# Seven-product tiles: product 1 copied into the next bank and accumulated on, products in another order

## The chip, the cores and the metric

The kernel runs on 1 core of one Trainium2 chip. The metric is the device time of one execution in microseconds, lower is better. Engines are named as in the profile: PE (TensorE matmul), PEld (its weight loads), DVE (VectorE), ACT (ScalarE), POOL (GpSimd), SP (SyncE, which issues the weight loads from memory).

## The reference, cut

A streaming encoder of two layers on 640 tokens (512 of a prompt, 8 streams of 16), width 1024, all in fp32. Each layer is a half SwiGLU feed-forward, a token mixer (retention in the first layer, stick-breaking attention in the second), a second half SwiGLU, and a gated per-layer embedding. The change lies in the up-projections of the feed-forward:

```python
def half_swiglu(x, g, w_gu, w_down):          # D_MODEL 1024, D_FF 2816
    h = rmsnorm(x, g) @ w_gu
    a, b = jnp.split(h, 2, axis=-1)
    return x + 0.5 * ((jax.nn.silu(a) * b) @ w_down)
```

It is called four times (`w_ffn_a` and `w_ffn_b` of both layers).

## The kernel before, in words

Activations lie transposed in SBUF: 128 partitions, 8 blocks of the model width, 640 token columns (`TOK`), which are handled as two halves of 320 (`HALF`). A matmul of fp32 precision is made of three in fp32r: each operand is split into a high part (ScalarE copies it, rounding: `w_hi`, `x_hi`, `g_hi`) and a low part (VectorE subtracts: `w_lo`, `x_lo`, `g_lo`), and high x high, high x low and low x high are summed in PSUM.

A feed-forward works through its 22 blocks of hidden units in four pieces of 4, 6, 6 and 6 (`PIECES`). For a piece it computes the blocks' `silu(a) * b`, then 8 down-projections (`KT`) that add the piece to `x`. The first piece uses plain products (L481). The other three use seven products in place of eight, in Winograd's form of Strassen's scheme: for a tile the 2x2 blocks are (gate weights, up weights) x (two halves of the model width) against (two halves of the width) x (two halves of the tokens). A tile is one block of 128 hidden units with both its gate and its up part. `winograd(piece)` runs six tiles, one after the other; there are 3 stages in each of 4 feed-forwards, 12 stages and 72 tiles. A product is 12 matmuls of 128x128 by 320 columns (4 blocks of width x 3 splits), all issued by `product` at L547. Operands of products 5, 6 and 7 are sums of weight blocks (`w_sum`, VectorE's `s1_s2`, `s3`, `s4`) and of activation blocks (`t_hi`, `t_lo`); each weight block, summed or not, is split again by ScalarE (`hi12`, `hi56`, `hi7`, `hi3`, `hi4`) and VectorE (`lo12`, `lo56`, `lo7`, `lo3`, `lo4`) just ahead of its product.

A tile has three PSUM banks, `x`, `y` and `v`, and the next tile the other bank pairs; the outputs are made so:

- product 1 into `x`; product 2 into `v`; the first result (gate, first half of tokens) is their sum: ScalarE's `snap1` copies `x` to SBUF, VectorE's `c11` adds `v` to it
- product 6 adds to `x`; `snap2` copies that (products 1 + 6) to SBUF
- product 5 into `y`; `snap3` copies it; product 7 adds to `x`, and `c22` adds `snap3`'s copy: the up part, second half
- product 3 adds to `y`, and `c12` adds `snap2`'s copy: the gate part, second half; product 4 adds to `x`: the up part, first half
- `silu` over all 640 columns, `gated` multiplies by the up part (two multiplications of 320 columns each), `ghi` and `glo` split the result for the down-projections

Products 3 and 4 of a tile are issued inside the next tile (`third(old)`, `fourth(old)`), so a middle tile's order on TensorE is 1, 2, 3old, 6, 4old, 5, 7; the first tile of a stage has 1, 2, 6, 5, 7; behind the last one stand its own 3 and 4.

Each engine runs a program written out by hand, in order; engines wait for each other by semaphores only. A wait stops all that stands behind it in the same engine's queue. ScalarE's queue in a tile is snap1, hi12 (of the next tile), hi3, snap2, silu (old), hi4, ghi (old), snap3, hi56 and hi7 (next). VectorE's is c22 (old), lo56, lo7, s1_s2 (next), c11, s3 (next), lo12 (next), c12 (old), lo3, gated (old), s4 (next), lo4, glo (old). Raw weights come by DMA into a ring of four slots (`raw`); SP issues slot n when the low split of slot n - 4 is done (`s_wlo`), so lo7 and lo4 release loads. Product 1 of a tile waits for `s_free`, which `gated` of the tile before increments.

Lines of the profile that matter: L547 the products; L481 the ordinary matmuls; L1071 snap1, L1076 snap2, L1080 snap3, L1084 silu, L1040 hi12, L1061 hi3, L1065 hi4; L1688 c11, L1693 c12, L1698 and L1700 gated, L1639 s1_s2, L1655 lo12, L1675 lo4; L1561 the low split of ordinary weights, L1566 that of activations.

Of the kernel before, what the change touches and what calls it, by code (L numbers as in the profile page):

```python
# [30 lines left out]
TOK = SEQ + STREAMS * STEP  # L31
TT = TOK // P
HALF = TOK // 2
# [19 lines left out]
CREDIT = 4  # L53
# [145 lines left out]
def trunk(nc, phases, xT, pT, gains, wst, ones_d, ident_d, negtri_d, cs_d, dec_d, rmask_d, smask_d, gpow_d,  # L199
          bmask_d, bcap_d, st_d, kc_d, vc_d, y_o, stp_o, sts_o, k_o, v_o):  # L200
    F, R = mybir.dt.float32, mybir.dt.float32r
    ALU, ACT = mybir.AluOpType, mybir.ActivationFunctionType
# [3 lines left out]
    with ctx:  # L206
        def sb(name, shape, dt=F, on=ctx):
            return on.enter_context(nc.sbuf_tensor(name, shape, dt))


        x = sb("x", [P, KT, TOK])
# [8 lines left out]
        scr = sb("scr", [P, 4, TOK])  # L220
# [68 lines left out]
        def sem(name):  # L289
            return ctx.enter_context(nc.semaphore(name))  # L290
# [16 lines left out]
        s_silu, s_sig, s_gate, s_tri = sem("s_silu"), sem("s_sig"), sem("s_gate"), sem("s_tri")  # L307
# [5 lines left out]
        s_free = sem("s_free")  # L313
        s_turned = sem("s_turned")
        s_wlo, s_xlo, s_rstd, s_glo, s_plo = sem("s_wlo"), sem("s_xlo"), sem("s_rstd"), sem("s_glo"), sem("s_plo")
        s_sr, s_xup, s_out = sem("s_sr"), sem("s_xup"), sem("s_out")
        s_rt, s_rot, s_kvs = sem("s_rt"), sem("s_rot"), sem("s_kvs")
# [4 lines left out]
        s_prod = {n: sem(f"s_prod{n}") for n in (1, 2, 3, 5, 6, 7)}  # L322
        s_read = sem("s_read")
        s_snap1, s_snap2, s_snap3 = sem("s_snap1"), sem("s_snap2"), sem("s_snap3")
        s_hi12, s_hi56, s_hi3, s_thi = sem("s_hi12"), sem("s_hi56"), sem("s_hi3"), sem("s_thi")
        s_lo12, s_lo56, s_lo3, s_tlo = sem("s_lo12"), sem("s_lo56"), sem("s_lo3"), sem("s_tlo")
        s_sum = [sem(f"s_sum{n}") for n in range(1, 5)]
        s_c11, s_c12, s_c22 = sem("s_c11"), sem("s_c12"), sem("s_c22")
        s_xn, s_t = sem("s_xn"), sem("s_t")

        s_apart, s_unshift = sem("s_apart"), sem("s_unshift")
# [61 lines left out]
        def w_block(wide, extra, n):  # L393

            return wide[:, n // 2, BLK * (n % 2):BLK * (n % 2 + 1)] if n < 4 else extra[:, n - 4, :]
# [10 lines left out]
        def b_side(product, whole, extra):  # L406

            at_x = {1: (0, 0), 2: (1, 0), 3: (1, 1), 4: (0, 1)}
            return quarter(whole, *at_x[product]) if product < 5 else extra[:, product - 5, :, :]
# [63 lines left out]
        def _(pe):  # L473
# [45 lines left out]
            def ffn(c):  # L519
# [19 lines left out]
                def product(n, out, start):  # L539

                    at = {1: 4, 2: 5, 3: 3, 4: 2, 5: 0, 6: 1, 7: 6}[n]
                    wh, wl = w_block(w_hi, wx_hi, at), w_block(w_lo, wx_lo, at)
                    xh, xl = b_side(n, x_hi, t_hi), b_side(n, x_lo, t_lo)
                    for k in range(4):
                        w = slice(k * P, (k + 1) * P)
                        for q, (a, b) in enumerate(((wh, xh), (wh, xl), (wl, xh))):
                            last = nc.tensor.matmul(out, a[:, w], b[:, k, :], start=start and k == 0 and q == 0,  # L547
                                                    stop=k == 3 and q == 2, skip_group_check=True)
                    return last

                def split_up_to(operand):

                    order = ("T1", "T3", "T2", "B11", "B21", "B22", "T4")
                    pe.wait_ge(s_tlo, CREDIT + 7 * (c["g"] // sum(PIECES)) + order.index(operand) + 1)

                def third(d):

                    pe.wait_ge(s_lo3, CREDIT + d["q"] + 1)
                    pe.wait_ge(s_snap3, CREDIT + d["q"] + 1)
                    product(3, d["y"], False).then_inc(s_prod[3], 1)  # L560
# [7 lines left out]
                def winograd(piece):  # L568
                    old = None
                    for d in fast_pairs(c, piece):  # L570
                        start_of = piece == 1 and d["first"]
                        pe.wait_ge(s_lo12, CREDIT + d["q"] + 1)
                        pe.wait_ge(s_free, CREDIT + c["unit"] + 1 + d["m"] - 2)
                        if start_of:
                            split_up_to("B11")
                        product(1, d["x"], True).then_inc(s_prod[1], 1)
                        if start_of:
                            split_up_to("B21")
                        product(2, d["v"], True).then_inc(s_prod[2], 1)
                        if old:  # L580
                            if old["first"] and piece == 1:
                                split_up_to("B22")
                            third(old)
                        pe.wait_ge(s_lo56, CREDIT + d["q"] + 1)
                        pe.wait_ge(s_snap1, CREDIT + d["q"] + 1)
                        product(6, d["x"], False).then_inc(s_prod[6], 1)
                        if old:
                            if old["first"] and piece == 1:
                                split_up_to("T4")
                            fourth(old)  # L590
                        product(5, d["y"], True).then_inc(s_prod[5], 1)
                        pe.wait_ge(s_wlo, CREDIT + c["n"] + d["m"] + 1)
                        pe.wait_ge(s_snap2, CREDIT + d["q"] + 1)
                        product(7, d["x"], False).then_inc(s_prod[7], 1)
                        old = d
                    third(old)
                    fourth(old)
# [365 lines left out]
        def _(act):  # L963
# [44 lines left out]
            def ffn(c):  # L1008
# [58 lines left out]

                def snap1(d):
                    act.wait_ge(s_prod[1], CREDIT + d["q"] + 1)
                    act.wait_ge(s_c11, CREDIT + d["q"])  # L1070
                    nc.scalar.activation(scr[:, 2, HALF:TOK], d["x"], ACT.Copy).then_inc(s_snap1, 1)  # L1071

                def snap2(d):
                    act.wait_ge(s_prod[6], CREDIT + d["q"] + 1)
# [5 lines left out]
                    nc.scalar.activation(scr[:, 2 + d["par"], 0:HALF], d["y"], ACT.Copy).then_inc(s_snap3, 1)  # L1080

                def silu(d):
                    act.wait_ge(s_c12, CREDIT + d["q"] + 1)
                    nc.scalar.activation(scr[:, d["par"], :], scr[:, d["par"], :], ACT.Silu).then_inc(s_silu, 1)  # L1084

                def ghi(d):
                    act.wait_ge(s_free, CREDIT + o + d["m"] + 2)
# [457 lines left out]

        @block.vector
        def _(dve):
            for s in (*s_sum, s_lo12, s_lo56, s_lo3, s_tlo, s_c11, s_c12, s_c22, s_xn, s_t, s_turned, s_free, s_wlo, s_xlo, s_rstd, s_glo, s_plo, s_sr, s_xup, s_out, s_rt, s_rot, s_kvs,
                      s_aggr, s_gn, s_ylo, s_sp, s_llo, s_cap, s_gated):
                dve.sem_inc(s, CREDIT)  # L1550
            tt, ts, stt = nc.vector.tensor_tensor, nc.vector.tensor_scalar, nc.vector.scalar_tensor_tensor
# [42 lines left out]
            def ffn(c):  # L1594
# [86 lines left out]
                    out = scr[:, 2 + d["par"], 0:HALF]  # L1681
                    tt(out, d["x"], out, ALU.add).then_inc(s_c22, 1)

                def c11(d):
                    dve.wait_ge(s_prod[2], CREDIT + d["q"] + 1)
                    dve.wait_ge(s_snap1, CREDIT + d["q"] + 1)
                    dve.wait_ge(s_glo, CREDIT + d["f"] - 1)
                    tt(scr[:, d["par"], 0:HALF], d["v"], scr[:, 2, HALF:TOK], ALU.add).then_inc(s_c11, 1)  # L1688

                def c12(d):  # L1690
                    dve.wait_ge(s_prod[3], CREDIT + d["q"] + 1)
                    dve.wait_ge(s_snap2, CREDIT + d["q"] + 1)
                    tt(scr[:, d["par"], HALF:TOK], d["y"], scr[:, 3, HALF:TOK], ALU.add).then_inc(s_c12, 1)  # L1693

                def gated(d):
# [11 lines left out]
                def winograd(piece):  # L1707
                    ds = fast_pairs(c, piece)
                    for i, d in enumerate(ds):
                        old = ds[i - 1] if i else None  # L1710
                        new = None if d["last"] else ds[i + 1]
                        if old:
                            c22(old)
                            lo56(d)
                            lo7(d)
                        if new:
                            s1_s2(new)
                        c11(d)
                        if new:
                            s3(new)  # L1720
                            lo12(new)
                        if old:
                            c12(old)
                        lo3(d)
                        if old:
                            gated(old)
                        if new:
                            s4(new)
                        lo4(d)
                        if old:  # L1730
                            glo(old)
                    c22(d)
                    split_lo(c, d["m"], 0, 0)
                    c12(d)
                    gated(d)
                    split_lo(c, d["m"] + 1, 0, 0)
                    glo(d)

                for nf_at, nf in enumerate(PIECES):
                    gbase = c["g"] + sum(PIECES[:nf_at])  # L1740
                    if nf_at == 0:
# [5 lines left out]
                        for j in range(2 * PLAIN):  # L1747
                            k = j // 2 % 2
                            f = c["g"] + j // 2
# [642 lines left out]
```

## Time and profile before

| | us |
|---|---|
| median of 3 runs | 2835.91 (2835.61 to 2838.54) |
| profiled execution, its own time | 2835.6 |
| its span, first to last instruction | 2834.0 |
| PE busy | 2786.3 (98%) |
| DVE busy | 1765.9 (62%) |
| ACT busy | 1136.2 (40%) |
| mean granted clock of PE | 0.997 of full speed |

The span is what the views of the trace cover; the profiled execution's own time is 1.6 us longer. In a timeline row the first number is the start in us from the span's start, the second how long it took; `x2` behind a row means that two such instructions in a row were merged. The name in front of `<-` is what is written, the names behind it are what is read. In square brackets stands how long the engine was idle before it, and who ended that. Matmuls overlap in the engine: one is listed with 0.31 us, while the next one starts 0.15 us after it.

### The profile page before, as it was taken

What the parts mean: (1) busy time and instruction counts of PE and PEld (TensorE: products, weight loads), DVE (VectorE), ACT (ScalarE), POOL (GpSimd) and SP (SyncE); (2) the same over time, 40 slices, a digit from 0 to 9 for tenths busy, and PEclk for the clock granted to TensorE, in tenths of its full rate; (3) what the DMA queues carried; (4) which work ended last, traced back from release to release, by engine and by line L of the source; (5) the groups of instructions that cost most, each with busy time, mean ns of one, the idle gap of its engine ahead of it and who ended that gap; (6) DMA issues with size and microseconds to landing.
All of it is one profiled execution on the core that took longest, in us unless ns stands there. A gap on an engine that the chain in (4) does not pass through costs nothing.

```text
span 2834.0 us, 47424 instructions
## 1 busy us (share of the span) xinstructions
PE 2786.3 (98%) x19234; PEld 2741.1 (97%) x19234; DVE 1765.9 (62%) x2471; ACT 1136.2 (40%) x1465; POOL 189.6 (7%) x190
## 2 busy tenths in 40 slices
PE   8999999999999999999999999999999999999997
PEld 8999999999999999999999999999999989999997
DVE  7757565546464677576657757564555567665755
ACT  5434343323232444343434434344534544433443
POOL 0000003111010100000110000002000010000021
PEclk9999999999999999999999999999999999999998
DMA  3322224233332313222321222223222212222221
GB/s 118 94 83 76 80 82 130 95 112 113 94 123 79 113 51 99 77 86 80 93 80 53 90 82 82 83 78 123 87 82 93 70 54 79 77 88 83 76 91 59
DMA packets 72704, 246.81 MB, mean 87 GB/s; under 512 B 8464, under 2 KB 8736, under 8 KB 71488
## 3 DMA queue, kind: packets, MB, share of 16 engines
q1 hardware_dynamic: 63216, 204.67, 23.4%
q0 software_dynamic: 9296, 39.40, 4.0%
q8 instruction: 142, 2.33, 0.3%
q14 instruction: 50, 0.41, 0.1%
HBM read 226.74 MB, written 17.30 MB: 86 GB/s over the span
## 4 chain that ended last, share of the span: by engine, by line
PE 90%; DVE 7%; issue 2%; ACT 1%; DMA 0%; ACTq 0%; SPq 0%; DVEq 0%
PE ps L481 40%; PE ps L547 31%; PE ps L820 7%; PE ps L696 4%; PE ps L873 2%; DVE w_lo L1561 1%; DVE xn L1600 1%; PE ps L794 1%; PE ps L907 1%; ACT w_hi L976 1%; DVE t_lo L1627 1%; PE ps L857 1%; PE ps L761 0%; DVE scr L1759 0%; DVE scr L1762 0%
## 5 line engine op out<-in xcount | busy, mean ns | idle before, releaser
L976 ACT ACTIVATE w_hi<-raw 128x1024 fp32r<-128x1024 f32 (+2 forms) x274 | 255.3, 932 | 742.7 <-PE ps L481 606.5
L1561 DVE TENSOR_TENSOR w_lo<-raw,w_hi 128x1024 fp32r<-128x1024 f32 (+2 forms) x274 | 297.3, 1085 | 99.5 <-ACT w_hi L976 91.3
L481 PE MATMUL ps<-g_hi,w_hi 128*128 128x320 f32 x1408 | 320.8, 308 | 7.2 <-DVE w_lo L1561 7.2
L481 PE MATMUL ps<-g_lo,w_hi 128*128 128x320 f32 x1408 | 319.9, 308 | 0.0
L481 PE MATMUL ps<-g_hi,w_lo 128*128 128x320 f32 x1408 | 319.7, 307 | 0.0
L481 PE MATMUL ps<-x_hi,w_hi 128*128 128x320 f32 x1216 | 285.0, 316 | 15.9 <-DVE x_lo L1566 12.0
L1791 DVE SCALAR_TENSOR_TENSOR x<-ps,x 128x640 f32<-128x640 f32 x128 | 105.4, 824 | 280.6 <-PE ps L481 280.6
L481 PE MATMUL ps<-x_hi,w_lo 128*128 128x320 f32 x1216 | 278.2, 310 | 0.0
L481 PE MATMUL ps<-x_lo,w_hi 128*128 128x320 f32 x1216 | 278.1, 310 | 0.0
L481 PEld LDWEIGHTS ps<-g_hi,w_hi 128*128 128x128 f32 x1408 | 234.6, 187 | 9.3 <-DVE w_lo L1561 9.3
L481 PEld LDWEIGHTS ps<-g_lo,w_hi 128*128 128x128 f32 x1408 | 235.0, 187 | 0.0
L481 PEld LDWEIGHTS ps<-g_hi,w_lo 128*128 128x128 f32 x1408 | 234.8, 187 | 0.0
L481 PEld LDWEIGHTS ps<-x_hi,w_hi 128*128 128x128 f32 x1216 | 204.5, 189 | 21.4 <-DVE w_lo L2204 8.5
L481 PEld LDWEIGHTS ps<-x_lo,w_hi 128*128 128x128 f32 x1216 | 204.4, 189 | 0.0
L481 PEld LDWEIGHTS ps<-x_hi,w_lo 128*128 128x128 f32 x1216 | 204.3, 189 | 0.0
L547 PE MATMUL ps<-x_hi,w_lo 128*128 128x320 f32 x576 | 177.9, 309 | 0.0
L547 PE MATMUL ps<-x_hi,w_hi 128*128 128x320 f32 x576 | 177.9, 309 | 0.0
L547 PE MATMUL ps<-x_hi,wx_lo 128*128 128x320 f32 x576 | 177.8, 309 | 0.0
L547 PE MATMUL ps<-x_lo,wx_hi 128*128 128x320 f32 x576 | 177.8, 309 | 0.0
L547 PE MATMUL ps<-x_hi,wx_hi 128*128 128x320 f32 x576 | 177.6, 308 | 0.0
L547 PE MATMUL ps<-x_lo,w_hi 128*128 128x320 f32 x576 | 177.5, 308 | 0.0
L547 PE MATMUL ps<-t_lo,w_hi 128*128 128x320 f32 x576 | 177.3, 308 | 0.0
(280 smaller groups left out, 6451.1 us busy)
## 6 DMA issues: line engine op xcount, KB each, us to landing
raw<-wst SPq DMA_DIRECT2D x292, 512.0 KB, 3.6
raw<-wst SPq DMA_DIRECT2D x96, 384.0 KB, 3.1
raw<-wst SPq DMA_DIRECT2D x32, 256.0 KB, 2.6
s<-st_d POOLq DMA_DIRECT2D x8, 1024.0 KB, 5.1
sts_o<-s POOLq DMA_DIRECT2D x16, 512.0 KB, 3.6
rd<-dec_d POOLq DMA_DIRECT2D x8, 640.0 KB, 5.7
kc<-kc_d POOLq DMA_DIRECT2D x8, 512.0 KB, 4.7
vc<-vc_d POOLq DMA_DIRECT2D x8, 512.0 KB, 6.0
```

The lines of the kernel that those rows point to most:

```text
L481: last = nc.tensor.matmul(out[:, h, :], a, b[:, HALF * h:HALF * (h + 1)], start=start and q == 0, stop=stop and q == 2, skip_group_check=True)
L547: last = nc.tensor.matmul(out, a[:, w], b[:, k, :], start=start and k == 0 and q == 0, stop=k == 3 and q == 2, skip_group_check=True)
L696: last = nc.tensor.matmul(out, a, b[:, p, w], start=part == 0 and k == 0 and q == 0 and t % 2 == 0, stop=part == 1 and k == 3 and q == 2, ...
L794: return nc.tensor.matmul(z[:, z0:z0 + w], bk[rows, par, b * P:(b + 1) * P], bq[rows, par, b * P:end], start=start, stop=False, skip_group ...
L820: last = nc.tensor.matmul(ps[:, sb_banks(use)[0], 0:HALF], a, b[:, xb, cols], start=n == 0 and q == 0, stop=n == len(blocks) - 1 and q == 2)
L857: last = nc.tensor.matmul(by_stream(zf(1)[:, Z_PAST:Z_NEW], s), kc[:, par, s, :], bqs[:, s, :, :], start=False, stop=s == STREAMS - 1, ski ...
L873: last = nc.tensor.matmul(z[:, z0 + P * (b2 - b):z0 + ZW[b]], tri[:, int(b2 > b), :], src[:, from_piece, from_col:from_col + ZW[b2]], star ...
L907: last = nc.tensor.matmul(ps[rows, 0, b * P:SEQ], bv[:, par, b, rows], e[:, at_piece, z0:z0 + ZW[b]], start=b == 0, stop=b == 3, skip_grou ...
L976: nc.scalar.activation(w_hi[:, (c["n"] + m) % 2, 0:cols], raw[:, r, 0:cols], ACT.Copy).then_inc(s_whi, 1)
L1561: tt(w_lo[:, p, 0:cols], raw[:, r, 0:cols], w_hi[:, p, 0:cols].bitcast(F), ALU.subtract).then_inc(s_wlo, 1)
L1600: stt(out=xn[k // 4][:, k % 4, :], in0=x[:, k, :], scalar=gain[:, c["norm"], k:k + 1], in1=rstd[:], op0=ALU.mult, op1=ALU.mult).then_inc(s ...
L1791: stt(out=xd, in0=acc(u), scalar=0.5, in1=xd, op0=ALU.mult, op1=ALU.add).then_inc(s_free, 1)
```

## The change

ScalarE's `snap1` writes its copy of product 1 not to SBUF but into bank `v`. Product 2 doesn't start a new sum there; it adds to that copy (`False` in place of `True`), and waits for `snap1`. So bank `v` holds the first result when product 2 is done: `c11` and its semaphore are gone, and `snap1` no longer waits for the `c11` of the tile before. `silu` becomes two instructions of 320 columns: one reads bank `v` and needs product 2, one works on `c12`'s result. The wait for `s_glo` (that the `scr` buffer is free) moves from `c11` to the first silu and to `c12`. The products' order becomes 1, 3old, 2, 6, 4old, 5, 7 in a tile that has an old one, and 1, 5, 2, 6, 7 in the first tile of a stage.

```diff
                         product(1, d["x"], True).then_inc(s_prod[1], 1)
-                        if start_of:
-                            split_up_to("B21")
-                        product(2, d["v"], True).then_inc(s_prod[2], 1)
+
+                        def second():
+
+                            if start_of:
+                                split_up_to("B21")
+                            pe.wait_ge(s_snap1, CREDIT + d["q"] + 1)
+                            product(2, d["v"], False).then_inc(s_prod[2], 1)
+
+                        def fifth():
+                            pe.wait_ge(s_lo56, CREDIT + d["q"] + 1)
+                            product(5, d["y"], True).then_inc(s_prod[5], 1)
+
+                        def sixth():
+                            pe.wait_ge(s_lo56, CREDIT + d["q"] + 1)
+                            pe.wait_ge(s_snap1, CREDIT + d["q"] + 1)
+                            product(6, d["x"], False).then_inc(s_prod[6], 1)
+
                         if old:
                             if old["first"] and piece == 1:
                                 split_up_to("B22")
                             third(old)
-                        pe.wait_ge(s_lo56, CREDIT + d["q"] + 1)
-                        pe.wait_ge(s_snap1, CREDIT + d["q"] + 1)
-                        product(6, d["x"], False).then_inc(s_prod[6], 1)
-                        if old:
+                            second()
+                            sixth()
                             if old["first"] and piece == 1:
                                 split_up_to("T4")
                             fourth(old)
-                        product(5, d["y"], True).then_inc(s_prod[5], 1)
+                            fifth()
+                        else:
+                            fifth()
+                            second()
+                            sixth()
                         pe.wait_ge(s_wlo, CREDIT + c["n"] + d["m"] + 1)
                         pe.wait_ge(s_snap2, CREDIT + d["q"] + 1)
                         product(7, d["x"], False).then_inc(s_prod[7], 1)
...
                 def snap1(d):
                     act.wait_ge(s_prod[1], CREDIT + d["q"] + 1)
-                    act.wait_ge(s_c11, CREDIT + d["q"])
-                    nc.scalar.activation(scr[:, 2, HALF:TOK], d["x"], ACT.Copy).then_inc(s_snap1, 1)
+                    nc.scalar.activation(d["v"], d["x"], ACT.Copy).then_inc(s_snap1, 1)
...
                 def silu(d):
+                    act.wait_ge(s_prod[2], CREDIT + d["q"] + 1)
+                    act.wait_ge(s_glo, CREDIT + d["f"] - 1)
+                    nc.scalar.activation(scr[:, d["par"], 0:HALF], d["v"], ACT.Silu)
                     act.wait_ge(s_c12, CREDIT + d["q"] + 1)
-                    nc.scalar.activation(scr[:, d["par"], :], scr[:, d["par"], :], ACT.Silu).then_inc(s_silu, 1)
+                    late = scr[:, d["par"], HALF:TOK]
+                    nc.scalar.activation(late, late, ACT.Silu).then_inc(s_silu, 1)
...
-                def c11(d):
-                    dve.wait_ge(s_prod[2], CREDIT + d["q"] + 1)
-                    dve.wait_ge(s_snap1, CREDIT + d["q"] + 1)
-                    dve.wait_ge(s_glo, CREDIT + d["f"] - 1)
-                    tt(scr[:, d["par"], 0:HALF], d["v"], scr[:, 2, HALF:TOK], ALU.add).then_inc(s_c11, 1)
-
                 def c12(d):
                     dve.wait_ge(s_prod[3], CREDIT + d["q"] + 1)
                     dve.wait_ge(s_snap2, CREDIT + d["q"] + 1)
+                    dve.wait_ge(s_glo, CREDIT + d["f"] - 1)
                     tt(scr[:, d["par"], HALF:TOK], d["y"], scr[:, 3, HALF:TOK], ALU.add).then_inc(s_c12, 1)
...
                         if new:
                             s1_s2(new)
-                        c11(d)
                         if new:
                             s3(new)
                             lo12(new)
```

## Rows read from the trace of the kernel before

**Rows 1.** page, sections 1 (busy us, share) and 4 (the chain).

```profile
PE 2786.3 (98%) x19234; PEld 2741.1 (97%) x19234; DVE 1765.9 (62%) x2471; ACT 1136.2 (40%) x1465; POOL 189.6 (7%) x190
...
PE 90%; DVE 7%; issue 2%; ACT 1%; DMA 0%; ACTq 0%; SPq 0%; DVEq 0%
```

**Rows 2.** waits of TensorE: engine, line, releaser: us in total, times, longest us.

```profile
PE ps L481 <- DVE x_lo L1566: 12.0, 3, 8.5
PE ps L481 <- DVE w_lo L1561: 10.1, 12, 1.5
```

**Rows 3.** L547's own view: nothing stands between its lines on idle and waiters.

```profile
its engine sat idle before it (us, times) until:
who waited for it (us, times):
```

**Rows 4.** stretches, L547 alone: us, PE and PEld busy (count), granted clock, DMA, GB/s.

```profile
101.23:175.08 73.85, 73.85 (x504) 73.75 (x504) 1.00 0.26 78
...
2626.49:2700.34 73.85, 73.85 (x504) 73.75 (x504) 1.00 0.25 74
```

**Rows 5.** timeline of a middle tile: start, us, engine, line, out<-in [idle before <-releaser].

```profile
146.95 0.31 PE L547 MATMUL ps<-x_hi,wx_hi 128*128 128x320 f32 x1
...
150.75 1.06 ACT L1040 ACTIVATE wx_hi<-raw 128x1024 fp32r<-128x1024 f32 x1 [1.40 <-PE ps L547]
...
151.84 1.23 DVE L1655 TENSOR_TENSOR wx_lo<-raw,wx_hi 128x1024 fp32r<-128x1024 f32 x1
...
152.98 0.48 DVE L1693 TENSOR_TENSOR scr<-ps,scr 128x320 f32<-128x320 f32 x1
...
154.18 0.44 ACT L1076 ACTIVATE scr<-ps 128x320 f32<-128x320 f32 x1 [1.07 <-PE ps L547]
...
154.51 0.73 ACT L1084 ACTIVATE scr<-scr 128x640 f32<-128x640 f32 x1
...
156.01 0.49 DVE L1700 TENSOR_TENSOR scr<-ps,scr 128x320 f32<-128x320 f32 x1 [0.24 <-PE ps L547]
```

**Rows 6.** timeline of ScalarE in the first tile of the first stage.

```profile
103.19 0.44 ACT L1071 ACTIVATE scr<-ps 128x320 f32<-128x320 f32 x1 [4.14 <-PE ps L547]
...
105.03 1.07 ACT L1040 ACTIVATE wx_hi<-raw 128x1024 fp32r<-128x1024 f32 x1 [1.40 <-PE ps L547]
...
106.00 0.62 ACT L1061 ACTIVATE w_hi<-w_sum 128x512 fp32r<-128x512 f32 x1
...
106.71 0.44 ACT L1076 ACTIVATE scr<-ps 128x320 f32<-128x320 f32 x1
```

**Rows 7.** timeline of TensorE in the same tile.

```profile
102.85 0.31 PE L547 MATMUL ps<-x_hi,wx_lo 128*128 128x320 f32 x1
...
106.36 0.31 PE L547 MATMUL ps<-t_hi,w_lo 128*128 128x320 f32 x1
...
106.51 0.31 PE L547 MATMUL ps<-t_hi,w_hi 128*128 128x320 f32 x1
```

**Rows 8.** timeline around a wait of TensorE for w_lo.

```profile
1053.38 0.69 DVE L1561 TENSOR_TENSOR w_lo<-raw,w_hi 128x512 fp32r<-128x512 f32 x1 [1.32 <-ACT w_hi L976]
...
1054.13 0.57 PE L481 MATMUL ps<-g_hi,w_hi 128*128 128x320 f32 x2 [0.80 <-DVE w_lo L1561]
...
1054.54 0.45 PE L481 MATMUL ps<-g_lo,w_hi 128*128 128x320 f32 x2
```

**Rows 9.** timeline of the tile whose load was latest.

```profile
2523.65 0.69 DVE L1639 TENSOR_TENSOR w_sum<-raw 128x512 f32<-128x512 f32 x1 [2.03 <-DMA raw<-wst]
...
2528.00 0.44 ACT L1076 ACTIVATE scr<-ps 128x320 f32<-128x320 f32 x1 [2.63 <-DVE scr L1693]
```

**Rows 10.** TensorE after two idles (timeline), and the stretch from 2311 (PEclk eighth).

```profile
74.70 0.56 PE L481 MATMUL ps<-g_hi,w_hi 128*128 128x320 f32 x2 [1.51 <-DVE w_lo L1561]
...
2311.50 0.90 PE L481 MATMUL ps<-x_hi,w_hi 128*128 128x320 f32 x2 [2.16 <-DVE x_lo L1566]
...
2311.00:2315.00 4.00, 3.50 (x11) 2.96 (x12) 0.44 (x1) 1.06 (x1) 0.00 (x0) 0.57 0.48 135
```

More of the change, by code:

```diff
@@ L327, in trunk @@
         s_sum = [sem(f"s_sum{n}") for n in range(1, 5)]
-        s_c11, s_c12, s_c22 = sem("s_c11"), sem("s_c12"), sem("s_c22")
+        s_c12, s_c22 = sem("s_c12"), sem("s_c22")
         s_xn, s_t = sem("s_xn"), sem("s_t")
@@ L1547, in _ @@
         def _(dve):
-            for s in (*s_sum, s_lo12, s_lo56, s_lo3, s_tlo, s_c11, s_c12, s_c22, s_xn, s_t, s_turned, s_free, s_wlo, s_xlo, s_rstd, s_glo, s_plo, s_sr, s_xup, s_out, s_rt, s_rot, s_kvs,
+            for s in (*s_sum, s_lo12, s_lo56, s_lo3, s_tlo, s_c12, s_c22, s_xn, s_t, s_turned, s_free, s_wlo, s_xlo, s_rstd, s_glo, s_plo, s_sr, s_xup, s_out, s_rt, s_rot, s_kvs,
                       s_aggr, s_gn, s_ylo, s_sp, s_llo, s_cap, s_gated):
```

## The prediction

> **What bounds the kernel now.** I read the page's busy table first: TensorE is busy 2786.3 of 2834.0 us, VectorE 1765.9, ScalarE 1136.2 [rows 1]. So TensorE's queue is the kernel, and only two things can move the time: how many matmul slots there are (the change keeps every product) and where that queue stands still. The list of what TensorE waited for comes next. Its largest rows are 12.0 us for x_lo and 10.1 us for w_lo, both at L481, the ordinary projections [rows 2]; no entry names L547, the line of the seven-product matmuls, and that line's own view lists nothing that its engine sat idle for [rows 3]. The table by stretches says it harder: a stage of six tiles has 6 x 7 x 12 = 504 matmuls and takes 73.85 us, in the first stage and in the last [rows 4]. 73.85 / 504 = 0.1465 us from start to start, and a product is 12 x 0.1465 = 1.76 us. There are 12 such stages (3 in each of 4 FFNs), 72 tiles in all. Within them the change has nothing to win from waits, since there are none. It can only keep that, or open one.
>
> **The change, part by part.** I number time from the start of product 1 of a tile.
>
> (a) *Removed: VectorE's c11*, 72 adds of 0.49 us (the add at L1693 has the same shape and took 0.48 us [rows 5]), some 35 us of VectorE. It does not lie on the path: TensorE never waited in these stages. Worth 0 us. The silu in two halves costs ScalarE about 72 x (2 x 0.44 - 0.73) = 11 us; 0.73 is the whole silu (154.51), 0.44 a 320-column copy (103.19) [rows 5, 6]. ScalarE is 40% busy; 0 us as long as the slack below holds.
>
> (b) *Product 2 now waits for snap1*, the copy of product 1 into the next bank. ScalarE started the old copy at 103.19, 0.34 us after the last matmul of product 1 started at 102.85, and took 0.44 us [rows 6, 7]. So it is done 0.78 us after that start, and TensorE meanwhile has a whole other product to do (3 of the old tile, or 5 in the first tile of a stage): 1.76 us of cover for 0.78 us. No row of before has ScalarE writing into a PSUM bank; the nearest is this copy out of one, at 0.44 us. It would have to take more than twice as long to show: from 0.44 to about 1.3 us it costs 0. I take 0.44 and 0. If the cover were gone, it would cost what (d) works out, in every tile. The Trainium skill ("ScalarE: Activation LUTs", the note that ScalarE to PSUM is faster than to SBUF) calls PSUM the lower-latency destination; by it, too, the copy would stay hidden, and no row here shows it.
>
> (c) *Middle tiles (60): order 1, 3old, 2, 6, 4old, 5, 7 in place of 1, 2, 3old, 6, 4old, 5, 7.* Products 6, 4old, 5 and 7 keep their places. 3old moves up by 1.76 us; it needs lo3 and snap3 of the old tile, which were done in the tile before. Product 2 moves down by 1.76 us, and with it hi12 of the next tile, which stands in ScalarE's queue behind the wait for product 2. Queued behind hi12 are hi3, snap2, silu, hi4, ghi, snap3, hi56, hi7; behind its lo12 on VectorE are c12, lo3, gated, s4, lo4, glo. I shift the tile whose product 1 started at 146.95 [rows 5]. hi12 started at 3.80 (150.75), now 3.80 + 1.76 = 5.56. It takes 1.06, then lo12 1.23 (151.84): done at 7.9. c12, which had started at 6.03 (152.98), now starts at 7.9 and ends at 8.4. snap2 had started at 7.23 (154.18) on the end of product 6; it also waits for c12 and now ends at 8.8. Product 7 wants it at 6 x 1.76 = 10.55: 1.7 us to spare. The second half of silu ends near 9.5, gated's last product, which was at 9.06 to 9.55 (156.01), near 10.5, and product 1 of the next tile wants it at 12.31: 1.8 us to spare. lo4 slips by about 1 us and the raw load that it releases with it; s1_s2, which waits for the load, has some 2 us before lo12 needs it. Sum: 0 us for 60 tiles.
>
> (d) *First tile of a stage (12): order 1, 5, 2, 6, 7 in place of 1, 2, 6, 5, 7.* Here the cover moves. Product 7 adds to the bank that product 6 filled and waits for snap2, the copy of that bank. Before, product 5 (1.76 us) lay between 6 and 7; now 7 stands directly behind 6. Last matmul of 6 starts at 106.36; snap2 starts at 106.71 and takes 0.44, so ends at 107.15 [rows 6, 7]. TensorE restarts 0.06 us after its releaser: w_lo ended at 1053.38 + 0.69 = 1054.07 and the matmul started at 1054.13 [rows 8]. So product 7 would start at 107.21 instead of 106.51: 0.70 us. The first pair of matmuls after a wait takes 0.41 us to the next (1054.13 to 1054.54) where a pair takes 0.29: 0.12 more. 0.82 us for each tile. Is ScalarE free in time? Product 2's last matmul now starts 1.76 before product 6's; before, that matmul started at 102.85 + 1.76 = 104.61, hi12 0.42 behind it at 105.03, hi3 0.97 later and 0.62 long [rows 6, 7]. So hi3 ends about 2.0 us behind it, and snap2 wants to start at 2.1 (1.76 + 0.35). It just fits, and if it didn't, the miss would be some 0.1 to 0.3 us a tile. Bounds: 0.6 (if part of restart and refill overlaps) to 1.1. I take 0.82.
>
> *Sum.* 12 x 0.82 = 9.8 us on top of the profiled execution's own 2835.6 us (span 2834.0): 2845.4. The median of the runs, 2835.91, is 0.3 above that execution, so I say 2845.7, 0.35% slower.
>
> **Rivals.**
>
> *R1, not slower: the matmuls themselves run faster.* 0.1465 us for 320 columns is more than 320 / 2.4 GHz = 0.133 us. If some of the 0.013 comes from VectorE and ScalarE reading PSUM beside TensorE, one read less (c11) could give it back. It decides at 9.8 / 6048 = 1.6 ns a matmul; twice that would give 2836 - 9.8 = 2826. Against it: both stages of [rows 4] come to the same 73.85 us, and VectorE, at other phases in the first tile than in the later ones, leaves no mark in them. Chance 0.03.
>
> *R2, the change doesn't do what the order says:* something else hides snap2 in the first tile, and nothing shows: 2836. It would need snap2 to start before product 6 ends, which its wait excludes. Chance 0.04.
>
> *R3, slower than forecast: the slack in (c) is not there.* Late loads are the likeliest way in. In one tile s1_s2 waited 2.03 us for its load and snap2 then 2.63 us, starting at 2528.00; product 7 would want it by about 2529.7 [rows 9]. In the first tile of a stage lo4 slips by 1.7 us (hi4 stands behind snap2, and product 6 ends 1.76 later), TensorE by 0.8, so the load for the third tile comes 0.9 later. With c11 out of the queue the late tile would have snap2 done at 9.6 of 10.55, so 0.9 us is left. If it fails in the 12 second tiles by 0.5 us: 6 us, 2851. If it fails in all 60 by 0.3 us: 18 us, 2863. It decides at 0.9 us more lateness than the worst tile of before. Chance 0.09 and 0.03.
>
> *R4, the clock falls.* The 12 new stalls leave TensorE idle for about 0.5 us each. After an idle of 2.16 us the first pair of matmuls took 0.90 us, and the mean granted clock of the 4 us from 2311 on was 0.57, a mixture of the two levels of 1.2 and 2.4 GHz; after 1.51 us idle the first pair took 0.56, so the clock had not fallen [rows 10]. Lost each time: 4 x (1 - 0.57) = 1.7 us; 12 x 1.7 = 20 us, 2866. It decides at an idle somewhere between 1.51 and 2.16 us, so 0.5 speaks against it. Chance 0.02. The Trainium skill ("TensorE: Matmul & The Clock Gate", section "A second HAM failure mode: psum-queue depth-cycling") says that small idles between groups of matmuls that wait on PSUM can make the clock swing between its two levels; that is this rival, and by that page's rule the time would be the 2866 above.
>
> **How the numbers follow.** Forecast (12 stalls of 0.6 to 1.1 us, all else hidden) 0.79, R1 0.03, R2 0.04, R3 0.12, R4 0.02. The forecast alone spans 12 x 0.6 = 7 to 12 x 1.1 = 13 us, 2843 to 2849. Runs of before reach from 2835.61 to 2838.54, which I add above, and the small form of R3 lies at 2851; below I add 2 us. Range 2841 to 2852. A measurement of this kernel can tell about 0.2% (5.7 us) from no change, so the border is 2841.6. Slower: 0.79 x 0.97 + 0.12 + 0.02 = 0.90, less a little for what I don't see: 0.88. Faster: half of R1 and the same unseen: 0.03. Same: 0.09.
>
> **What would show it.** In the profile after: 12 waits of TensorE's product line for ScalarE's snap2, about 0.5 us each, 6 us in all, and none for snap1 or for c12; each stage 73.85 + 0.8 = 74.65 us; the matmul pitch 0.1465 and the granted clock unchanged; snap1 0.44 us or less. Wrong it would be if L547's successor waited for snap1 (then (b) is mis-sized), if waits stood in tiles other than the first (R3), or if a stage took 73.85 (R1, R2).

## The result, and the profile after

The changed kernel takes 2848.14 us (median, 2847.19 to 2849.37) against 2835.91 before: ratio 1.0041, 95% interval 1.003 to 1.0053, five executions of each (the table ahead of the prediction says three for before). Forecast were 2845.7 us and 0.35% slower, with 2841 to 2852 as range. The profiled execution took 2847.79 us, with a span of 2846.2 against 2834.0.

The page of the changed kernel, section 1 (busy us, share of the span, instructions), beside [rows 1]:

```profile
PE 2791.1 (98%) x19234; PEld 2742.1 (96%) x19234; DVE 1738.2 (61%) x2399; ACT 1123.8 (39%) x1537; POOL 188.6 (7%) x190
```

VectorE has 72 instructions less and 27.7 us less of busy time. ScalarE has 72 more; its two silu lines take 34.0 and 31.1 us where the one took 52.6, and its busy time is still 12.4 us lower, since more of its instructions now stand back to back and overlap, and overlaps count once. Neither moved the end. What TensorE waited for (engine, line, releaser: us in total, times, longest), beside [rows 2, 3]:

```profile
PE ps L481 <- DVE x_lo L1585: 12.3, 3, 8.8
PE ps L481 <- DVE w_lo L1580: 10.1, 12, 1.5
PE ps L547 <- ACT scr L1091: 7.4, 12, 0.6
```

The two old rows are where they were. The third is new: the product line waits 12 times, 7.4 us together, for L1091, which is snap2. There is no row for L1086, snap1's copy into PSUM. The stretches of the first and the last stage, product line alone (us, PE and PEld busy, granted clock, DMA, GB/s), beside [rows 4]:

```profile
100.48:175.21 74.73, 74.11 (x504) 73.78 (x504) 1.00 0.26 76
2638.43:2713.16 74.73, 74.11 (x504) 73.78 (x504) 1.00 0.25 73
```

504 matmuls as before, in 74.73 us instead of 73.85: 0.88 us for each stage, in every one of the 12, with the clock at 1.00. 12 x 0.88 = 10.6 of the 12.2 us between the spans. The place, in the timeline of TensorE and ScalarE in the first tile of the first stage, beside [rows 6, 7]:

```profile
107.37 0.30 PE L547 MATMUL ps<-t_hi,w_lo 128*128 128x320 f32 x1
108.29 0.38 PE L547 MATMUL ps<-t_hi,wx_hi 128*128 128x320 f32 x1 [0.62 <-ACT scr L1091]
108.51 0.31 PE L547 MATMUL ps<-t_lo,wx_hi 128*128 128x320 f32 x1
...
102.44 0.42 ACT L1086 ACTIVATE ps<-ps 128x320 f32<-128x320 f32 x1 [4.13 <-PE ps L547]
...
107.00 0.61 ACT L1077 ACTIVATE w_hi<-w_sum 128x512 fp32r<-128x512 f32 x1
107.71 0.44 ACT L1091 ACTIVATE scr<-ps 128x320 f32<-128x320 f32 x1
```

Product 6's last matmul starts at 107.37, snap2 at 107.71 and ends at 108.15, product 7 starts at 108.29. The idle of 0.62 us in the wait rows counts from the modelled end of the last matmul, so it is less than what is lost. From start to start it is 0.92 us where 0.15 is usual, and the next start follows after 0.22 for 0.15: 0.84 of the 0.88 us. hi3 (L1077) ends at 107.61, 0.1 us before snap2, so ScalarE was free just in time.

The other 1.6 us stand outside the stages. Between the ninth stage and the tenth, where the attention lies, before took 495.52 us and after 498.50: 3.0 us more; the stretch ahead of the first stage and the one behind the last were 0.75 and 0.62 us shorter. The stretches of after that hold the 3.0 us, and the same two in a second profiled execution of the same kernel (us, busy of PE, PEld, DVE, ACT, POOL, then granted clock, DMA, GB/s):

```profile
2292.00:2296.00 4.00, 4.00 (x17) 1.52 (x16) 0.58 (x2) 0.54 (x2) 0.00 (x0) 0.58 0.36 120
2320.00:2327.00 7.00, 6.63 (x23) 5.84 (x24) 2.27 (x3) 2.63 (x3) 0.00 (x0) 0.56 0.23 78
```

```profile
2292.00:2296.00 4.00, 3.10 (x19) 1.53 (x20) 1.42 (x4) 0.60 (x3) 0.00 (x0) 1.00 0.40 131
2320.00:2327.00 7.00, 6.83 (x25) 6.03 (x26) 2.27 (x4) 2.63 (x3) 0.00 (x0) 0.59 0.28 78
```

In the first execution the mean granted clock was 0.58 from 2292 to 2296, where the second has 1.00: 4 x 0.42 = 1.7 us. The low stretch at 2320 is the one behind TensorE's long wait in [rows 10]; it now lasts some 7 us instead of 4, in both executions, 7 x 0.44 - 4 x 0.43 = 1.4 us. `e7` below has it long too (0.64 from 2312 to 2319) and takes the time of before. I take both for a matter of where an execution's clock happens to fall, not of the change; `after_again` below tests the stretch at 2292.

### The profile page after: what moved, and what is told of

Read it like the earlier page. It is cut to its first block, busy times and chain, and to the rows that moved or that the text cites. A ratio compares the mean times of both kernels' runs of the same rounds, so it can differ in the third digit from the quotient of the medians.

```text
span 2846.2 us, 47355 instructions
## 1 busy us (share of the span) xinstructions
PE 2791.1 (98%) x19234; PEld 2742.1 (96%) x19234; DVE 1738.2 (61%) x2399; ACT 1123.8 (39%) x1537; POOL 188.6 (7%) x190
## 4 chain that ended last, share of the span: by engine, by line
PE 90%; DVE 7%; issue 2%; ACT 2%; DMA 0%; ACTq 0%; SPq 0%; DVEq 0%
PE ps L481 40%; PE ps L547 31%; PE ps L836 7%; PE ps L712 4%; PE ps L889 2%; DVE w_lo L1580 1%; DVE xn L1619 1%; PE ps L810 1%; PE ps L923 1%; ACT w_hi L992 1%; DVE t_lo L1646 1%; PE ps L873 1%; PE ps L777 0%; DVE scr L1772 0%; DVE scr L1775 0%
## 5 line engine op out<-in xcount | busy, mean ns | idle before, releaser
L547 PE MATMUL ps<-x_hi,w_hi 128*128 128x320 f32 x576 | 178.5, 310 | 0.0
L547 PE MATMUL ps<-x_hi,w_lo 128*128 128x320 f32 x576 | 177.9, 309 | 0.0
L547 PE MATMUL ps<-x_lo,wx_hi 128*128 128x320 f32 x576 | 177.8, 309 | 0.0
L547 PE MATMUL ps<-x_hi,wx_hi 128*128 128x320 f32 x576 | 177.7, 309 | 0.0
L547 PE MATMUL ps<-x_lo,w_hi 128*128 128x320 f32 x576 | 177.6, 308 | 0.0
L547 PE MATMUL ps<-x_hi,wx_lo 128*128 128x320 f32 x576 | 177.4, 308 | 0.0
L547 PE MATMUL ps<-t_lo,w_hi 128*128 128x320 f32 x576 | 177.1, 308 | 0.0
```

## Experiments

All of them change the changed kernel, save `e2`, which changes the kernel before.

**The order alone.** The kernel before with only the first tile reordered:

```diff
+                        if not old:
+                            pe.wait_ge(s_lo56, CREDIT + d["q"] + 1)
+                            product(5, d["y"], True).then_inc(s_prod[5], 1)
                         if start_of:
                             split_up_to("B21")
                         product(2, d["v"], True).then_inc(s_prod[2], 1)
...
                             fourth(old)
-                        product(5, d["y"], True).then_inc(s_prod[5], 1)
+                            product(5, d["y"], True).then_inc(s_prod[5], 1)
```

> The kernel before, with c11 and its own middle tiles, but the first tile of a stage in the order 1, 5, 2, 6, 7. Theory: 12 waits for snap2 of about 0.62 us, each stage 74.73 us, time 2835.9 + 12 x 0.88 = 2846.5 (2845.5 to 2848). Rival A (the accumulation on ScalarE's copy is what costs): stages at or near 73.85 and 2836 to 2838.

Measured: 2845.24 us, ratio 1.0031 (1.0019 to 1.0043), stages of 74.70 us, and this row among TensorE's waits:

```profile
PE ps L547 <- ACT scr L1079: 7.4, 12, 0.6
```

L1079 is snap2 there. The time is 0.3 us under the forecast band, in six executions that spread from 2843.63 to 2848.80; the stages and the waits decide, and by them the theory holds. With c11, the copy to SBUF and the old middle tiles all in place, the order of the first tile alone makes the same 12 waits. Between 74.70 and 74.73 lie 0.03 us a stage, 0.4 us in all, for the rest of the change.

**Cover for both copies.** In the first tile product 2 goes between 6 and 7:

```diff
                             fifth()
-                            second()
                             sixth()
+                            second()
...
                         snap1(d)
-                        if new:
+                        if old and new:
                             hi12(new)
                         hi3(d)
                         snap2(d)
+                        if new and not old:
+                            hi12(new)
```

> The changed kernel with the first tile of a stage in the order 1, 5, 6, 2, 7: product 5 covers the copy of product 1, product 2 covers snap2; ScalarE does hi12 of the next tile behind snap2 in that tile. Theory (the whole loss is TensorE standing still for snap2 in 12 first tiles, 0.88 us each): no wait of the product line is left, each stage takes 73.85 us, and the time is that of the kernel before, 2836 (2835.5 to 2839). Rival A (some of the loss, about 1.6 us of the 12.2 between the two spans, comes from the copy into PSUM or from the products' new order in the middle tiles): stages still above 73.85, or 2837.5 and more in every run. Rival B (the freed VectorE time is worth something once the stall is gone): below 2835.

Measured: 2849.55 us, ratio 1.0045 (1.0031 to 1.0059), stages of 74.88. A miss for the theory and for rival B. What rival A gave as its sign is there, stages above 73.85, but not by its cause, and the waits say why (and the first matmul of the second tile):

```profile
PE ps L547 <- DVE wx_lo L1676: 8.9, 12, 0.7
...
110.81 0.41 PE L547 MATMUL ps<-x_hi,wx_hi 128*128 128x320 f32 x1 [0.74 <-DVE wx_lo L1676]
```

The wait for snap2 is gone, and product 1 of the second tile waits for lo12 (L1676) instead. hi12 may overwrite its buffer only when product 2 is done, and product 2 had just moved to 1.76 us ahead of product 7's end. From there hi12 (from 108.44, 1.06 us) and lo12 (1.23 us, to 110.76) follow one another, longer than the 1.76 us of product 7. The stall had moved; for this order I had not followed what the end of product 2 releases, as the prediction does for the middle tiles.

**The same, with hi12 and lo12 cut in two behind the first tile**, so that product 1's half doesn't hang on product 2:

```diff
+                def hi1(d):
+                    whole(d)
+                    nc.scalar.activation(wx_hi[:, 0, :], raw_blocks(c, d["m"])[:, 0, :], ACT.Copy).then_inc(s_hi1, 1)
+
+                def hi2(d):
+                    act.wait_ge(s_prod[2], CREDIT + d["q"])
+                    nc.scalar.activation(wx_hi[:, 1, :], raw_blocks(c, d["m"])[:, 3, :], ACT.Copy).then_inc(s_hi12, 1)
...
+                        if new and not old:
+                            hi1(new)
                         hi3(d)
                         snap2(d)
                         if new and not old:
-                            hi12(new)
+                            hi2(new)
...
-                            lo12(new)
+                            if old:
+                                lo12(new)
+                            else:
+                                lo1(new, stage_no(c, piece))
```

> The order of e1 (1, 5, 6, 2, 7 in the first tile of a stage), and the next tile's double weight split hi12 / lo12 is cut in two in that one place: the half for product 1 is made as soon as product 1 of the first tile has released its buffer, the half for product 2 behind product 2. Theory (e1 lost because product 1 of the second tile waited for a low split that was chained to product 2; the copy into PSUM itself costs nothing): no wait of the product line is left, stages of 73.85 us, time 2836 (2834.5 to 2838.5), the same as before. Rival A (the copy into PSUM or the order in the middle tiles costs something by itself): stages above 73.9. Rival B (35 us less of VectorE work is worth something): below 2834.5.

Measured: 2836.39 us against 2836.37 for before on the same chip, ratio 0.9998 (0.9989 to 1.0007). TensorE's waits name no product line, and the first stage reads:

```profile
101.29:175.16 73.87, 73.87 (x504) 73.77 (x504) 1.00 0.25 77
```

73.87 us: 12 x 0.02 = 0.2 us is all that the copy into PSUM and the middle tiles' order cost, and 33 us less on VectorE (1732.8 busy for 1765.9) bring nothing. The whole loss was the stall, and an order without it exists, but that kernel is no faster than the one before.

**No cover for snap1.** In the 60 middle tiles product 2 goes right behind product 1:

```diff
                         if old:
+                            second()
                             if old["first"] and piece == 1:
                                 split_up_to("B22")
                             third(old)
-                            second()
                             sixth()
```

> The changed kernel, but in the 60 middle tiles product 2 stands right behind product 1, as in the kernel before, so that its wait for the copy into PSUM has no product ahead of it. Theory: the same exposed copy as in the first tiles, 0.86 to 0.88 us in each of 60 tiles more, 12 + 60 = 72 waits, stages of 74.73 + 5 x 0.87 = 79.1 us, time 2848 + 52 = 2900 (2896 to 2904). Rival A (TensorE could start product 2 before the copy is done, or the copy into PSUM is much cheaper): below 2880. Rival C (the clock falls with many small idles): a mean granted clock well below 0.99 and over 2915.

Measured: 2893.37 us, ratio 1.02 (1.0185 to 1.0216), stages of 78.59. TensorE's waits, and TensorE and ScalarE around one of the new ones:

```profile
PE ps L547 <- ACT ps L1086: 30.7, 60, 0.5
...
PE ps L547 <- ACT scr L1091: 7.4, 12, 0.6
```

```profile
113.07 0.31 PE L547 MATMUL ps<-x_hi,wx_lo 128*128 128x320 f32 x1
113.89 0.41 PE L547 MATMUL ps<-x_hi,wx_hi 128*128 128x320 f32 x1 [0.51 <-ACT ps L1086]
...
113.42 0.42 ACT L1086 ACTIVATE ps<-ps 128x320 f32<-128x320 f32 x1 [1.07 <-PE ps L547]
```

60 waits as forecast, but 0.77 us a tile ((78.59 - 74.73) / 5) and not 0.87, so the time fell below the band. The parts: snap1 takes 0.42 us (0.44 for snap2), and from its end at 113.84 to product 2 it is 0.05 us, where after snap2 it is 0.14. Even with 72 idles the granted clock of the execution was 0.996: small idles don't pull the clock down here.

**Why 0.14 in one place and 0.05 in the other.** The two waits ahead of product 7, exchanged:

```diff
-                        pe.wait_ge(s_wlo, CREDIT + c["n"] + d["m"] + 1)
                         pe.wait_ge(s_snap2, CREDIT + d["q"] + 1)
+                        pe.wait_ge(s_wlo, CREDIT + c["n"] + d["m"] + 1)
                         product(7, d["x"], False).then_inc(s_prod[7], 1)
```

> The changed kernel with TensorE's two waits ahead of product 7 exchanged: first snap2 (the one that blocks), then the weights' low split (long done). The restart after a blocking wait differs by place: 0.14 us from the end of snap2 to product 7's first matmul in the changed kernel, 0.05 us from the end of snap1 to product 2 in e3 and from lo12 to product 1 in e1, where the blocking wait is the only or the first one. Theory G (it matters that the blocking wait is the second of two): restart 0.05 us, waits of 0.53, stages of 74.67. Theory H (it lies in what follows, the weights that product 7 loads, or in snap2): restart stays 0.14, waits 0.62, stages 74.73. Time 2846 to 2849 by either.

```profile
PE ps L547 <- ACT scr L1091: 6.3, 12, 0.5
...
107.75 0.44 ACT L1091 ACTIVATE scr<-ps 128x320 f32<-128x320 f32 x1
...
108.24 0.42 PE L547 MATMUL ps<-t_hi,wx_hi 128*128 128x320 f32 x1 [0.53 <-ACT scr L1091]
108.49 0.31 PE L547 MATMUL ps<-t_lo,wx_hi 128*128 128x320 f32 x1
```

snap2 ends at 107.75 + 0.44 = 108.19 and product 7 starts at 108.24: 0.05. Waits of 0.53, stages of 74.67, as theory G had it. The one execution took 2847.92 us, too coarse for 0.8 us.

**Half the copy.** snap2 of the first tile copies 160 columns (the rest of the second gate half of those tiles is computed with stale data):

```diff
-                    nc.scalar.activation(scr[:, 3, HALF:TOK], d["x"], ACT.Copy).then_inc(s_snap2, 1)
+                    n = HALF // 2 if d["first"] else HALF
+                    nc.scalar.activation(scr[:, 3, HALF:HALF + n], d["x"][:, 0:n], ACT.Copy).then_inc(s_snap2, 1)
```

> The changed kernel, but snap2 of the first tile of a stage copies 160 of the 320 columns, so the second gate half of those tiles is computed with stale data in the other 160. Theory (the stall is the copy's latency): the 160-column copy is shorter by 160 columns at ScalarE's pace of about 1 ns a column, so some 0.13 to 0.17 us less in each of the 12 waits: waits of about 0.47 us, stages of 74.58, time 2846 to 2847. Rival D (the stall is mostly a fixed cost of handing over and restarting): waits stay at 0.60 to 0.62 and the stage at 74.73.

Measured: 2844.99 us, ratio 1.0033 (1.0021 to 1.0045), stages of 74.60 (74.58 forecast); the time is 1 us under the forecast.

```profile
108.15 0.30 ACT L1092 ACTIVATE scr<-ps 128x160 f32<-128x160 f32 x1
...
108.60 0.38 PE L547 MATMUL ps<-t_hi,wx_hi 128*128 128x320 f32 x1 [0.49 <-ACT scr L1092]
```

The copy is 0.13 us shorter (0.30 for 0.44), so are the wait (0.49 for 0.62) and the stage. The stall follows the copy one to one; rival D falls.

**How much slack the middle tiles have.** Idle copies ahead of snap2 there, 2 and then 5:

```diff
+                    if not d["first"]:
+                        for _ in range(2):
+                            nc.scalar.activation(scr[:, 2, HALF:TOK], d["x"], ACT.Copy).then_inc(s_pad, 1)
+                            pads[0] += 1
+                            act.wait_ge(s_pad, pads[0])
```

> The changed kernel with 2 idle copies of 320 columns on ScalarE ahead of snap2 in the 60 middle tiles, each waited for, some 0.9 to 1.1 us together. Theory: snap2 of a middle tile is done 1.6 us before TensorE can want it (155.88 + 0.14 against 157.61), and the last product of gated 1.9 us before product 1 of the next tile: no new wait of the product line, stages of 74.73, 2846 to 2849. Rival R3 (the slack is not there): waits in middle tiles, over 2855.

> The same with 5 idle copies, some 2.2 to 2.7 us. Theory: the slack of 1.6 us is used up and product 7 of each of the 60 middle tiles waits for snap2 by 0.6 to 1.1 us, plus about 0.1 for the restart: stages of 74.73 + 5 x (0.7 to 1.2) = 78.2 to 80.7, time 2890 to 2920. Rival F (the slack is larger than the timeline shows, since TensorE's wait is put down late): no wait, 2848.

Measured, one execution each: 2846.22 us with stages of 74.73 for two copies (0.94 us of delay), 2902.76 with stages of 78.9 to 79.9 for five. With five, TensorE's waits for snap2 (L1097) and snap3 (L1101), one of the delays with the matmul that waits for it, and the longest wait with the load ahead of it:

```profile
PE ps L548 <- ACT scr L1097: 43.6, 60, 1.8
...
PE ps L548 <- ACT scr L1101: 4.8, 12, 0.4
...
159.78 2.31 ACT L1094 ACTIVATE scr<-ps 128x320 f32<-128x320 f32 x5 [1.24 <-DVE scr L1713]
162.13 0.44 ACT L1097 ACTIVATE scr<-ps 128x320 f32<-128x320 f32 x1
162.71 0.39 PE L548 MATMUL ps<-t_hi,wx_hi 128*128 128x320 f32 x1 [0.60 <-ACT scr L1097]
...
1923.86 0.69 DVE L1664 TENSOR_TENSOR w_sum<-raw 128x512 f32<-128x512 f32 x1 [2.24 <-DMA raw<-wst]
...
1930.43 0.39 PE L548 MATMUL ps<-t_hi,wx_hi 128*128 128x320 f32 x1 [1.80 <-ACT scr L1097]
```

The first idle copy starts at 159.78, snap2 at 162.13: 2.35 us later. Less the slack of 1.6 that is 0.75. Product 7 starts at 162.71, 0.90 us after the matmul ahead of it (161.81) where 0.15 is usual: 0.75 late, though its row lists 0.60 of idle.

The 60 waits are not the 60 middle tiles. Twelve are the first tiles' own, which have no idle copies and wait 0.62 us as before. The other 48 are the second to fifth tile of each stage: 34 of them list 0.58 to 0.62 us, as the slack says, and 14 list 0.70 to 1.80. Those 14 are the tiles, of the third to fifth, whose s1_s2 waited longest for its load (over 1.1 us), so late loads (R3's way in) do reach TensorE once the slack is gone. The sixth tile has no next tile, so snap2 comes earlier there and product 7 doesn't wait; the 12 waits for snap3, which stands behind snap2 in ScalarE's queue, stand ahead of its product 3.

**The changed kernel again.**

> The changed kernel once more, unchanged, beside the kernel before on the same chip. Theory: stages of 74.73 in every execution, so 10.6 us over before; the profiled execution of the first comparison showed 12.2 because the granted clock was low for 3.4 us more in two places outside the stages, which comes and goes: median 2845.5 to 2848.5, with a profile whose time outside the stages is between 1946.7 and 1950. Rival E (the change brings the clock's fall with it): the extra low stretch near 2290 us is there again and the median at 2848 or above.

Measured: 2847.01 us (2846.64 to 2847.64) against 2836.37, ratio 1.0035 (1.0022 to 1.0049), stages of 74.73. That is 10.64 us, where 12 x 0.88 is 10.56. The low stretch at 2292 us was not there (its rows stand above), so rival E falls: the change does not bring it each time. Whether it makes it more frequent stays open. The profiles of `e1`, `e3` and `e8` show such a stretch too (granted clock 0.58, 0.62 and 0.59 in the 4 us from 2293, 2329 and 2292); those of `e4`, `e5`, `e6` and `e7`, which copy into PSUM as well, do not, nor do the two without that copy, `before` and `e2`.

## Why the prediction was right, step by step

- *What bounds it.* Right: TensorE had no idle time in the stages, so nothing could be won there. `e7` takes the stall away and keeps all the rest, and comes out at 0.9998.
- *(a) c11 and the silu: 0 us.* Right (`e7`), for both.
- *(b) snap1 hidden under one product.* Right: no wait in the changed kernel. It takes 0.42 us into PSUM where I took 0.44. Uncovered it costs 0.77 us a tile (`e3`), not the 0.82 that I took over from (d). The Trainium skill ("ScalarE: Activation LUTs", the note that ScalarE to PSUM is faster than to SBUF) calls PSUM the shorter way. The trace agrees, by 16 ns (means of 422 ns for the new snap1 and 438 for the old).
- *(c) middle tiles: 0 us.* Right, and nearly to the row: snap2 was forecast to end 8.8 us behind product 1, and in the tile that starts at 147.06 it ends at 155.88:

```profile
155.44 0.44 ACT L1091 ACTIVATE scr<-ps 128x320 f32<-128x320 f32 x1 [1.23 <-DVE scr L1707]
...
157.62 0.31 PE L547 MATMUL ps<-t_hi,wx_hi 128*128 128x320 f32 x1
```

From its end to product 7 it is 1.74 us (1.7 forecast), the same to 0.01 us in the second to fifth tile of every stage, and 2.88 in the sixth. Less the restart of 0.14 that leaves 1.6, and `e5` and `e6` bear it out.
- *(d) first tiles: 12 x 0.82.* The mechanism and the count are right, and snap2 had ScalarE free in time, by 0.1 us; the size was 0.88 (`after_again`). The term too small is the restart: 0.14 us from the releaser to the matmul where I took 0.06 from a wait for w_lo. `e8` shows the reason. Partly made up by the refill, 0.22 us to the next matmul for 0.15, so 0.07 where I had 0.12. 0.34 + 0.44 + 0.14 - 0.15 + 0.07 = 0.84; of the 0.04 left, 0.03 is what `e2`, without the other edits, does not have.
- *The sum.* 9.8 forecast, 10.6 measured as the stall; the first comparison's medians are 12.2 apart, the second's 10.6, and what the first has more lies outside the stages, in its profiled execution in the low clock near 2292 and 2320. The median is 2.4 us above the forecast: 0.8 is the stall's size, 1.6 a term that the sum doesn't have. It still lies within the 2843 to 2849 of the stalls alone; the room added for scatter was needed for the slowest executions (2849.17 and 2849.37) only. In (d) two errors partly cancel by luck, the restart 0.08 too small and the refill 0.05 too large.
- *Rivals.* R1: the pitch of the matmuls is what it was, 73.87 / 504 = 0.1466 in `e7`, with c11 gone. R2: excluded by the waits. R3: the late loads came (VectorE's s1_s2 waited for its load in 48 tiles, 2.1 us at the longest; in 17 before), and none reached TensorE; in `e6`, with the slack used up, they did. R4: 12 idles of 0.62 and, in `e3`, 60 more of 0.51 left the clock at 1.00 in the stages and 0.996 to 0.997 over the execution. The case it was built on had more idle than it names: ahead of the 2.16 us in [rows 10] TensorE had stood still for 1.29 us at 2308.19. The Trainium skill ("TensorE: Matmul & The Clock Gate", section "A second HAM failure mode: psum-queue depth-cycling") says that small idles between groups of matmuls can make the clock swing. With the idles of this case, 72 at most, the trace doesn't bear that out, and the measurement decides.

## What to carry to other kernels

When an engine is busy 98% and a change only reorders its work, look at each pair of neighbours in the new order: does the later one wait for a copy of what the earlier one made? Each copy needs a piece of other work as cover, at both ends of a loop too, where the steady state's cover (the old tile's product) is missing. And moving a product moves what its end releases: `e1` cured one stall and made another of the same size, because a weight buffer was handed on by the product that had moved.

## What the runs showed of the hardware

Where two waits stand ahead of a matmul and the second is the one that blocks, TensorE restarts 0.14 us after the releaser's end; when the blocking one comes first (`e1`, `e8`) or alone (`e3`), 0.05 us. `e8` is one execution, the same in all 12 places: 6.3 us of waiting for 7.4. The restart is 0.09 us sooner, and the first matmul then takes 0.25 us to the next for 0.22, so 0.06 us is what stays of it each time (stages of 74.67 for 74.73). Putting the wait that blocks first is free.
